# Three normed outputs joined to the residual stream two tiles at a time, their g factors on ScalarE, weight splits reordered, and the output stored in four pieces

## The reference

```python
mix = jnp.concatenate([rms_norm_2(o_sb, ...), rms_norm_2(o_mla, ...)], axis=-1) @ w_o[i]
x = x + rms_norm_2(mix, g_post_mix[i])
h = rms_norm_2(x, g_pre_ffn[i])
u = causal_depthwise_conv(h @ w_up[i], conv_w[i], conv_b[i])
gate, val = jnp.split(u, 2, axis=-1)
f = (jax.nn.gelu(gate, approximate=True) * val) @ w_down[i]
x = x + rms_norm_2(f, g_post_ffn[i])
e = p[i] @ w_ple[i]
g = jax.nn.sigmoid(rms_norm_2(x, g_ple_gate[i]) @ w_ple_gate[i] + b_ple_gate[i])
x = x + rms_norm_2(g * e, g_post_ple[i])
```

## Time and profile before

| | |
|---|---|
| device time, median of 3 runs | 1212.28 us (1206.51 to 1212.61) |
| device time of the profiled execution | 1209.78 us |
| its span | 1208.0 us |
| TensorE matmul busy | 1088.4 us (90%) |
| VectorE busy | 774.3 us (64%) |
| ScalarE busy | 593.5 us (49%) |
| GpSimd busy | 184.6 us (15%) |
| granted TensorE clock, mean | 0.910 of full speed |
| the chain that ended last | TensorE 66%, VectorE 21%, ScalarE 8%, issue 3%, DMA 1% |

### The profile page before, as it was taken

How to read it: one execution, slowest core, us unless ns; L and a number is a source line. 1 busy time by engine, 2 the same in 40 slices (tenths; PEclk the granted TensorE clock), 3 DMA queues, 4 the chain that set the end, 5 groups by cost and what they waited for, 6 DMA issues and landing times.

```text
span 1208.0 us, 18421 instructions
## 1 busy us (share of the span) xinstructions
PE 1088.4 (90%) x7268; PEld 983.7 (81%) x7268; DVE 774.3 (64%) x1503; ACT 593.5 (49%) x1063; POOL 184.6 (15%) x85
## 2 busy tenths in 40 slices
PE   5996699999999997989999999979889799999865
PEld 5995489899989984768989998966668799999754
DVE  4899785656687335767475678532354778777655
ACT  5543365444554333545544445368344566545433
POOL 2771011212221000002112212120000000101100
PEclk9996799999999766799999999988779899999968
DMA  8441044545544340003354555410121255554400
GB/s 332 175 154 56 1 154 161 183 166 210 179 170 140 110 175 0 1 1 139 140 188 164 206 195 181 157 70 1 35 105 71 107 182 196 179 177 175 171 1 35
DMA packets 22405, 158.39 MB, mean 131 GB/s; under 512 B 2480, under 2 KB 2736, under 8 KB 3888
## 3 DMA queue, kind: packets, MB, share of 16 engines
q1 hardware_dynamic: 21456, 153.51, 35.0%
q10 hardware_dynamic: 864, 3.71, 0.8%
HBM read 156.16 MB, written 1.05 MB: 130 GB/s over the span
## 4 chain that ended last, share of the span: by engine, by line
PE 66%; DVE 21%; ACT 8%; issue 3%; DMA 1%; POOL 0%; ACTq 0%; DVEq 0%
PE bank L657 62%; DVE obank L1703 4%; DVE split_lo L551 4%; ACT split_hi L543 3%; PE obank L657 2%; ACT L1224 2%; PE bank L787 1%; DVE y L1703 1%; DVE x L1695 1%; ACT hidden_parts L1224 1%; DVE hidden_parts L1695 1%; ACT y L1224 1%; DVE square_sum L1695 1%; DVE mlp_lo L1703 1%; DVE act_parts L1703 1%
## 5 line engine op out<-in xcount | busy, mean ns | idle before, releaser
L657 PE MATMUL bank<-act_parts,split_hi 128*128 128x256 f32 (+1 forms) x1632 | 335.1, 303 | 29.3 <-DVE split_lo L551 13.0
L551 DVE TENSOR_TENSOR split_lo<-ring,split_hi 128x1024 fp32r<-128x1024 f32 (+1 forms) x206 | 267.3, 1307 | 134.6 <-ACT split_hi L543 134.3
L543 ACT ACTIVATE split_hi<-ring 128x1024 fp32r<-128x1024 f32 (+1 forms) x280 | 287.9, 1045 | 111.0 <-PE bank L657 109.0
L551 POOL TENSOR_TENSOR split_lo<-ring,split_hi 128x1024 fp32r<-128x1024 f32 (+1 forms) x74 | 181.5, 2459 | 983.1 <-ACT split_hi L543 983.1
L657 PEld LDWEIGHTS bank<-act_parts,split_hi 128*128 128x128 f32 x1632 | 269.4, 199 | 41.6 <-issue 23.3
L657 PE MATMUL bank<-hidden_parts,split_hi 128*128 128x512 f32 (+1 forms) x816 | 265.5, 377 | 4.2 <-POOL split_lo L551 3.1
L657 PE MATMUL bank<-act_parts,split_lo 128*128 128x256 f32 x880 | 255.5, 290 | 0.0
L657 PE MATMUL bank<-hidden_parts,split_lo 128*128 128x256 f32 x752 | 210.2, 280 | 0.0
L657 PEld LDWEIGHTS bank<-hidden_parts,split_hi 128*128 128x128 f32 x816 | 148.7, 188 | 35.8 <-POOL split_lo L551 3.7
L657 PEld LDWEIGHTS bank<-act_parts,split_lo 128*128 128x128 f32 x880 | 176.2, 200 | 0.0
L657 PE MATMUL bank<-mlp_hi,split_hi 128*128 128x256 f32 x512 | 146.1, 285 | 4.9 <-DVE mlp_lo L1703 2.5
(11 more groups left out here) (218 smaller groups left out, 1327.5 us busy)
## 6 DMA issues: line engine op xcount, KB each, us to landing
ring<-in_weights SPq DMA_DIRECT2D x141, 1024.0 KB, 4.8
ring<-in_weights SPq DMA_DIRECT2D x5, 768.0 KB, 4.0
x<-in_x ACTq DMA_DIRECT2D x1, 1024.0 KB, 7.7
y<-in_mem ACTq DMA_DIRECT2D x1, 1024.0 KB, 9.7
out<-x SPq DMA_DIRECT2D x1, 1024.0 KB, 3.9
consts<-in_consts ACTq DMA_DIRECT2D x1, 931.5 KB, 12.9
ring<-in_weights SPq DMA_DIRECT2D x1, 512.0 KB, 3.6
consts<-in_consts ACTq DMA_DIRECT2D x1, 260.0 KB, 7.7
```

Source lines behind the costliest of these rows:

```text
L543: nc.scalar.activation(split_hi[:, w % SPLIT, 0:n], src, ACT.Copy).then_inc(sem("high_parts"), 1)
L551: (nc.vector if engine == "vector" else nc.gpsimd).tensor_tensor(split_lo[:, w % SPLIT, 0:n], src, split_hi[:, w % SPLIT, 0:n].bitcast(F32 ...
L657: return nc.tensor.matmul(dst, lhsT, rhs, start=start, stop=stop)
```

## The change

1. In `post_norm` VectorE multiplies y by the factor straight out of the PSUM bank of `.bc`, two tiles (128x512) in one instruction, with the 256 columns of the factor repeated. It adds two tiles of y to x in one instruction, and the multiplication of the next pair stands ahead of the addition of the last, so that an addition no longer waits for the instruction just before it. Low halves and folds come pair by pair, one pair later. The copy to `rb` is gone; the bank of `.bc` is released by VectorE behind the folds of the third pair instead of by ScalarE's copy.
2. The factor g is applied by ScalarE. In the first join it is the scale of the copy that empties the bank; in the other two it is an instruction more for each tile, behind its square.
3. In the last chunk of "down", ScalarE's weight split of tile t stands ahead of the square of tile t for t = 0 to 5. The splits for t = 6 and 7 stand behind the root on ScalarE. On VectorE they stand behind the reciprocal, and the one for t = 5 is GpSimd's.
4. TensorE does ten bf16 products of 128x512 into the bank of postffn.stat ahead of that statistic.
5. The output is stored in four DMAs of 256 KB, each after its pair of tiles.

```diff
-            sp_.wait_ge(sem("result"), KD)
-            sp_.dma_start(out, flat(x[:, :, :])).then_inc(sem("stored"), 16)
-            sp_.wait_ge(sem("stored"), 16)
+            for t in range(0, KD, 2):
+                sp_.wait_ge(sem("result"), t + 2)
+                sp_.dma_start(out[:, SEQ * t:SEQ * t + 2 * SEQ], flat(x[:, t:t + 2, :])).then_inc(sem("stored"), 16)
+            sp_.wait_ge(sem("stored"), 16 * (KD // 2))
@@ tensor
             mlp("ffn", "up", "down", "ffn.hidden", UP_CHUNKS, 2, projected)
+            keep_busy(take("postffn.stat", 0), 10)
             folded_stat("postffn")
@@ scalar
-            def raw_outputs(stage, norm):
+            def raw_outputs(stage, norm, gname):
...
-                    copy(y[:, t, :], ps).then_inc(emptied(stage, t), 1)
+                    copy(y[:, t, :], ps, const(gname, t, 1)).then_inc(emptied(stage, t), 1)
...
             def squares_after(norm, after, between=None, raw=True):
-                keep_bcast(after)
...
                         if n == len(UP_CHUNKS):
                             if t % KD == KD - 3:
                                 load_root()
+                            if t % KD < KD - 2:
+                                pump("down", t)
                             wait_emptied(act, "down", t)
                             do(sq[:, t % KD, :], y[:, t % KD, :], ACT.Square).then_inc(sem("postffn.squares"), 1)
-                        pump("down", t)
+                            copy(y[:, t % KD, :], y[:, t % KD, :], const("g_postffn", t % KD, 1)).then_inc(sem("scaled_outputs"), 1)
+                        else:
+                            pump("down", t)
             root("postffn", 2, 1024)
+            for t in (2 * KD + 6, 2 * KD + 7):
+                pump("down", t)
...
                     do(sq[:, t - 1, :], y[:, t - 1, :], ACT.Square).then_inc(sem("postple.squares"), 1)
+                    if t < KD:
+                        copy(y[:, t - 1, :], y[:, t - 1, :], const("g_postple", t - 1, 1)).then_inc(sem("scaled_outputs"), 1)
             root("postple", 2, 1024)
-            keep_bcast("postple")
+            copy(y[:, KD - 1, :], y[:, KD - 1, :], const("g_postple", KD - 1, 1)).then_inc(sem("scaled_outputs"), 1)
@@ vector
-                wait_emptied(dve, f"{name}.bc", 0)
-                for t in range(KD):
-                    settle(stt(y[:, t, :], y[:, t, :], const(gname, t, 1), rb[:, :], ALU.mult, ALU.mult))
-                    tt_(x[:, t, :], x[:, t, :], y[:, t, :], ALU.add)\
-                        .then_inc(sem("result" if after is None else f"{name}.x"), 1)
...
+                wait_tile(dve, f"{name}.bc", 0)
+                factor = rows(bank(f"{name}.bc", 0)[:, 0:SEQ], 2)
+
+                def lows(first):
+                    for t in (first, first + 1):
                         if raw:
-                            low_of_x(t - 1, act_hi, act_lo, f"g_{after}", after)
-                        fold(after, t - 1)
+                            low_of_x(t, act_hi, act_lo, f"g_{after}", after)
+                        fold(after, t)
+
+                for t in range(0, KD + 2, 2):
+                    if t < KD:
+                        step(tt_(y[:, t:t + 2, :], y[:, t:t + 2, :], factor, ALU.mult))
+                    if t >= 2:
+                        dve.wait_ge(sem("vector_step"), own[0] - (1 if t < KD else 0))
+                        tt_(x[:, t - 2:t, :], x[:, t - 2:t, :], y[:, t - 2:t, :], ALU.add)\
+                            .then_inc(sem("result" if after is None else f"{name}.x"), 2)
+                    if t >= 4 and after is not None:
+                        lows(t - 4)
+                dve.sem_inc(emptied(f"{name}.bc", 0), 1)
                 if after is not None:
...
+                    lows(KD - 2)
...
-                        pump("down", t)
+                        if n < len(UP_CHUNKS) or t % KD < KD - 3:
+                            pump("down", t)
             fold("postffn", KD - 1)
+            pump("down", 2 * KD + 5)
             invert("postffn", 2)
-            post_norm("postffn", "g_postffn", None, "plegate")
+            for t in (6, 7):
+                pump("down", 2 * KD + t)
+            dve.wait_ge(sem("scaled_outputs"), KD)
+            post_norm("postffn", "plegate")
...
-            dve.wait_ge(sem("ple.gated"), KD)
-            post_norm("postple", "g_postple", None)
+            dve.wait_ge(sem("scaled_outputs"), 2 * KD)
+            post_norm("postple")
```

More of the change, by code:

```diff
@@ L1585, in squares_after @@
                         load_root()
-            raw_outputs("o", "postmix")
+            raw_outputs("o", "postmix", "g_postmix")
             squares_after("ffn", "postmix", lambda t: empty(("ple", t), q[:, t, :], bank("ple", t)[:, 0:SEQ]), raw=False)
@@ L2291, in _, with post_norm @@
             low(flat(act_lo[:, 4:8, :]), flat(mix[:, 4:8, :]), flat(act_hi[:, 4:8, :]), "o.act")
-            def post_norm(name, gname, stage, after=None, raw=True):
-                if stage:
-                    for t in range(KD):
-                        wait_emptied(dve, stage, t)
-                        pump(stage, t)
-                wait_emptied(dve, f"{name}.bc", 0)
-                for t in range(KD):
-                    settle(stt(y[:, t, :], y[:, t, :], const(gname, t, 1), rb[:, :], ALU.mult, ALU.mult))
-                    tt_(x[:, t, :], x[:, t, :], y[:, t, :], ALU.add)\
-                        .then_inc(sem("result" if after is None else f"{name}.x"), 1)
-                    if after is not None and t >= 1:
-                        if raw:
-                            low_of_x(t - 1, act_hi, act_lo, f"g_{after}", after)
-                        fold(after, t - 1)
+            def post_norm(name, after=None, raw=True):
+                wait_tile(dve, f"{name}.bc", 0)
+                factor = rows(bank(f"{name}.bc", 0)[:, 0:SEQ], 2)
+                def lows(first):
+                    for t in (first, first + 1):
+                        if raw:
+                            low_of_x(t, act_hi, act_lo, f"g_{after}", after)
[10 more added lines that the diff above has]
+                dve.sem_inc(emptied(f"{name}.bc", 0), 1)
                 if after is not None:
-                    if raw:
-                        low_of_x(KD - 1, act_hi, act_lo, f"g_{after}", after)
-                    fold(after, KD - 1)
+                    lows(KD - 2)
             for t in range(KD):
@@ L2316, in _ @@
             invert("postmix", 2)
-            post_norm("postmix", "g_postmix", None, "ffn", raw=False)
+            for t in range(KD):
+                wait_emptied(dve, "o", t)
+            post_norm("postmix", "ffn", raw=False)
             invert("ffn", 2)
```

## The result

| | before | after |
|---|---|---|
| device time, median of 9 runs each | 1211.8 us (1205.6 to 1219.5) | 1201.6 us (1198.4 to 1204.5) |
| profiled execution, span | 1208.0 us | 1199.8 us |

The ratio is 0.992, 95% interval 0.989 to 0.994: some 10 us less, against 12.2 forecast. 1201.6 us lies in the range, 3.6 us above the forecast.

A forecast was written before the change was run, and what follows sets the result against it. TensorE was taken to be two thirds of the chain, leaving gains at the three joins: 8.7 + 0.2 + 3.3 = 12.2 us off an average of 1210.3, giving 1198 us; range 1193 to 1203.

The forecast's parts named there:

- Sums, splits and statistic of the second join: Second join: statistic at 1145.9 instead of 1152.85, then two splits on VectorE; y starts 6.0 us earlier.
- C: Stretch from the end of the last "down" product to the second join's statistic; 9.26 us before, predicted 2.3.
- D: Stretch from the second join's statistic to the first multiplication of y; 3.25 us before, predicted 4.2.
- Unit costs: VectorE in the joins: 0.69 us per 128x512 instruction, 0.60 back to back; low half 0.40, fold 0.34.
- First join: First join: itself 2.1 us shorter, but TensorE stalls 2.4 us for the broadcast's bank; 0.2 us less.
- A: Stretch from the first join's statistic to the second statistic, behind ple; 12.83 us before, predicted 12.6.
- Clock in the second join: Slices nearly without a gap bring the clock's rise nearer to k = 7; 0.7 us less, bounds 0 and 2.
- F: Stretch from the second join's last low half to the plegate statistic, behind two ple_gate tiles; 5.75 us before, predicted 5.05.
- Third join: Third join: y starts 0.35 us earlier, two-tile instructions save 2.0, the store in quarters 1.0; sum 3.3.
- The first join did not gain: Rival: bank released no later than TensorE arrives, so the first join's 2.1 to 2.4 us come through; 1195.8 us, chance 0.12.
- the splits did not take the place of the old wait: Rival, second join: GpSimd's later split holds folds 6 and 7, ScalarE's splits slide too; 1202 us, chance 0.16.
- the slower one: Rival: clock stays low through all of ple_gate and two tiles of "up"; 1217.3 us, chance 0.04.

The follow-up runs named there:

- p_splits: Kernel before with only the new order of the last "down" weight splits and the ten products ahead of the second join's statistic; ratio to before 0.997.
- r_late: e_release with the weight splits of "down" tiles 6 and 7 moved behind the second join; ratio to the kernel before 0.9885.
- p_joins: Kernel after with the old order of the splits at the second join, without the ten products and with one store; ratio to before 0.999.
- p_store: Kernel before with only the output stored in four pieces of two tiles; ratio to before 0.999.
- e_release: Kernel after with the broadcast's bank given back by the last multiplication of y instead of behind fold 5; ratio to the kernel before 0.988.
- r_fillk: r_fill plus one more product in front of each of slices 1 to 7 of the first ple_gate tile; ratio to the kernel before 0.987.
- r_fill: e_release with 24 more products on TensorE between the second join's broadcast and the first ple_gate product; ratio to the kernel before 0.990.

## Why the prediction was right, and where it was wrong

- **Sums, splits and statistic of the second join: right.** C 2.54 instead of 2.3, D 4.16 instead of 4.2. GpSimd's hold and the second split as the last thing ahead of y came as written; p_splits shows the 6.2 us by themselves, r_late that it was the splits.
- **Unit costs: right.** The 128x512 instructions with a repeated factor in PSUM took 681 ns, those in SBUF 685; the row at 512 columns had said 0.69:

```profile
L1704 DVE TENSOR_TENSOR x<-x,y 128x512 f32<-128x512 f32 x12 | 8.1, 685 | 0.0
L1704 DVE TENSOR_TENSOR y<-y,bank 128x512 f32<-128x512 f32 x12 | 7.9, 681 | 1.8 <-PE bank L658 1.8
```

- **First join: the mechanism right, the size wrong.** TensorE stalled 2.47 us (2.4 predicted), and ple 5 started at 948.20, which less the 2.33 us by which this profile ran late is 945.87 (945.8 predicted). What failed is the step "ple 6 is done at 947.6": it priced ple 5 to 7 at full clock. They took 4.16 us instead of the 2.7 that twelve such products take at the pace of the first twenty (4.48 for 20), and the statistic came 1.0 us later than in the sum. The low clock is 0.7 of that: p_joins, with ple 5 to 7 at full clock, has A 12.97. The other 0.4 is missing from the sum even so; there ScalarE began its copy of ple 6 at 947.96 (949.66, less the 1.70 by which that profile ran late), against 947.6. The bound of 2.3 us more had named a low clock, but in the arrivals of "up", not in ple.
- **Clock in the second join: wrong by 0.65.** The step said that slices without a gap would bring the rise nearer to k = 7. They had nearly none and it did not: 4.1 us instead of 4.2. The distance is not set by the slices alone: in p_store it was 3.3 us with the code of before, in e_release 3.7 with that of after. In r_fillk F goes down by 1.5, when the clock doesn't fall in the first place.
- **Third join: right in its parts**, 0.42 us and 2.04 us for 0.35 and 2.0. The store gave 1.4 instead of 1.0: the line through a 144 KB and a 1 MB transfer put a quarter at 2.85 us, it landed in 2.4. The 144 KB were a load and not a store, so the line had little to rest on.
- **Total.** 10.5 of 12.2 us in like stretches; that H gave back what C, E and G missed is chance. The remaining distance of 1201.6 from 1198.0 is no larger than what varies ahead of the first statistic, 934.4 to 944.2 us, which the sum took as fixed. Two sums are off by 0.1: the release comes to 945.7 and not 945.8, and 6.0 and 1.9 us are 7.9 and not 8.0.
- **Rivals.** The first join did not gain (A 13.63); the splits did not take the place of the old wait (C 2.54, D 4.16); the slower one (the clock low through all of ple_gate) did not happen: 0.99 of full clock from 1168 on.

What stays open: why TensorE is at 1.2 GHz for 171 to 195 us ahead of the first join when the code there is the same, and what decides whether ple begins at 1.2 GHz.

## What to carry to other kernels

When a join is shortened, look for who holds the buffer that the other engine needs next: here one release, moved from behind the folds to the last reader, was worth 2.5 us where the clock stayed up, more than the 1.8 that the two-tile instructions brought in the second join. A wait that used to absorb a low clock is part of the price of removing it. And where run-to-run changes ahead of the edit are as large as its effect, cut the profiles at fixed marks and compare the stretches.

## What the runs showed of the hardware

- One product of 0.2 us ahead of each arriving slice kept TensorE at 2.4 GHz through the arrivals (r_fillk); work in all the time ahead of the slices, with nothing between them, did not (r_fill).
- The same instructions had ple at 7.25 or 9.4 us, 1.9 us of the whole, from one kernel to the next with no change near it.
- Ahead of the first join the same code was at 1.2 GHz for 171 to 195 us from one profile to the next, and its end moved from 934.4 to 944.2 us.
- A VectorE fold that began during a GpSimd subtraction took 2.06 us instead of 0.42 and ended 0.28 us behind it; sums with one input in PSUM beside it took their usual 0.44.
- A quarter of a 1 MB store landed in 2.4 us against 3.9: a fixed part of about 1.9 us, an estimate worked out from the two.
